# High and low input parts in one product of 512 moving columns, summed when a bank is taken

## The reference

```python
def conv_ffn(h, w_gu, conv_w, conv_b, w_down):
    a, u = jnp.split(h @ w_gu, 2, axis=-1)
    a = causal_depthwise_conv(a, conv_w, conv_b)
    return (jax.nn.silu(a) * u) @ w_down
...
o = from_q_groups(o) @ w_o          # the mixer's output projection
x = x + conv_ffn(h, ...)            # D_MODEL 1024, D_FF 2816
```

## Time and profile before

| | |
|---|---|
| median of 3 runs | 1273.48 us (1270.31 to 1273.67) |
| the profiled execution | 1273.24 us, of which the profiled span is 1271.4 us |
| busy in the span | PE 94%, weight loads 89%, DVE 60%, ACT 44%, POOL 36% |
| up steps of layer 0 | about 236 to 358 us of the span |
| down parts of layer 0 | about 358 to 422 us |
| the same of layer 1 | about 533 to 723 us |
| the same of the third | about 1058 to 1255 us |

### The profile page before, as it was taken

How to read it: one execution, slowest core, us unless ns; L and a number is a source line. 1 busy time by engine, 2 the same in 40 slices (tenths; PEclk the granted TensorE clock), 3 DMA queues, 4 the chain that set the end, 5 groups by cost and what they waited for, 6 DMA issues and landing times.

```text
span 1271.4 us, 23862 instructions
## 1 busy us (share of the span) xinstructions
PE 1195.2 (94%) x9313; PEld 1130.8 (89%) x9313; DVE 765.0 (60%) x1093; ACT 565.6 (44%) x788; POOL 452.6 (36%) x430
## 2 busy tenths in 40 slices
PE   6998999999999888999999999998988898999996
PEld 5987678999999875999999998988978896999996
DVE  5753564767655566676765464436755657777544
ACT  4232344554544444455454336644353444545432
POOL 4522232266630433166651211113431303666401
PEclk9998799999999989999999999998999999999998
DMA  6651001666645540466665453243341453667551
GB/s 200 205 192 41 9 26 34 200 176 188 188 160 183 164 134 2 120 178 187 177 197 182 149 173 127 69 129 104 101 133 34 148 165 87 191 174 196 180 169 50
DMA packets 224581, 175.49 MB, mean 138 GB/s; under 512 B 7796, under 2 KB 205788, under 8 KB 224380
## 3 DMA queue, kind: packets, MB, share of 16 engines
q1 hardware_dynamic: 219052, 168.33, 44.4%
q10 hardware_dynamic: 5424, 6.09, 1.4%
q0 software_dynamic: 32, 0.03, 0.0%
HBM read 173.39 MB, written 1.05 MB: 137 GB/s over the span
## 4 chain that ended last, share of the span: by engine, by line
PE 81%; DVE 8%; ACT 3%; issue 3%; POOL 3%; DMA 1%; SPq 0%; ACTq 0%; DVEq 0%; POOLq 0%
PE bank L574 22%; PE bank L580 22%; PE bank L575 21%; PE bank L840 2%; DVE w_l L1512 2%; ACT w_h L1157 2%; PE bank L608 2%; PE bank L614 1%; PE bank L704 1%; PE bank L1013 1%; PE bank L808 1%; POOL work L2261 1%; DVE work L1627 1%; PE bank L848 1%; PE bank L692 1%
## 5 line engine op out<-in xcount | busy, mean ns | idle before, releaser
L574 PE MATMUL bank<-xh,w_h 128*128 128x256 f32 (+2 forms) x1792 | 451.6, 289 | 5.5 <-DVE xl L1530 4.1
L575 PE MATMUL bank<-xl,w_h 128*128 128x256 f32 (+2 forms) x1792 | 443.0, 284 | 0.0
L574 PEld LDWEIGHTS bank<-xh,w_h 128*128 128x128 f32 x1792 | 339.9, 190 | 8.5 <-issue 5.1
L575 PEld LDWEIGHTS bank<-xl,w_h 128*128 128x128 f32 x1792 | 340.8, 190 | 1.0
L1512 DVE TENSOR_TENSOR w_l<-raw,w_h 128x2048 fp32r<-128x2048 f32 (+3 forms) x95 | 212.2, 2234 | 158.6 <-ACT w_h L1157 158.5
L1157 ACT ACTIVATE w_h<-raw 128x2048 fp32r<-128x2048 f32 (+3 forms) x95 | 173.3, 1825 | 241.7 <-PE bank L580 220.5
L580 PE MATMUL bank<-xh,w_l 128*128 128x256 f32 (+2 forms) x1792 | 251.4, 283 | 2.9 <-DVE w_l L1512 2.9
L580 PEld LDWEIGHTS bank<-xh,w_l 128*128 128x128 f32 x1792 | 230.5, 189 | 3.3 <-DVE w_l L1512 3.1
L2183 POOL TENSOR_TENSOR work<-work 128x256 f32<-128x256 f32 x66 | 162.9, 2469 | 140.4 <-ACT work L1300 140.4
L1795 DVE TENSOR_TENSOR w_l<-raw,w_h 128x2048 fp32r<-128x2048 f32 x66 | 151.4, 2293 | 14.0 <-ACT w_h L1296 13.8
L574 PE MATMUL bank<-hid_h,w_h 128*128 128x256 f32 (+1 forms) x592 | 148.0, 284 | 2.5 <-issue 1.8
(11 more groups left out here) (291 smaller groups left out, 1595.9 us busy)
## 6 DMA issues: line engine op xcount, KB each, us to landing
raw<-in_ffn_w_gu SPq DMA_DIRECT2D x88, 512.0 KB, 5.0
raw<-in_w_in SPq DMA_DIRECT2D x26, 1024.0 KB, 5.2
raw<-in_ffn_w_down SPq DMA_DIRECT2D x40, 512.0 KB, 4.6
raw<-in_w_ffn_up SPq DMA_DIRECT2D x22, 512.0 KB, 4.1
raw<-in_w_ffn_gate SPq DMA_DIRECT2D x22, 512.0 KB, 5.3
raw<-in_nsa_w_in SPq DMA_DIRECT2D x10, 1024.0 KB, 5.4
raw<-in_w_ffn_down SPq DMA_DIRECT2D x20, 512.0 KB, 4.4
raw<-in_swa_w_qkv SPq DMA_DIRECT2D x5, 1024.0 KB, 5.3
```

The costliest lines, as they stand in the source:

```text
L574: mm(dst, parts[0][:, k, cols], high, start=first, stop=False)
L575: mm(dst, parts[0][:, k, cols], low, start=False, stop=False)
```

## The change

Where a stage works on 256 tokens (both output projections of the first block, the up steps of its two layers, and the down parts of all three layers), one product moves 512 columns past each high block: the 256 high parts of x, and beside them the 256 low parts. They go to the two halves of the bank (`side_terms`). The low terms still move 256 columns and add to the left half. The high and low parts of x, of the attention output and of the hidden values are laid out so that one access pattern reaches both; sizes and places stay as they are. The other stages (the input projections, the third layer's up steps, the second block's output projections) keep two products.

Whoever takes a chunk now has to add the two halves, and one instruction of DVE may read only one operand of the accumulator memory here. In the up steps of layers 0 and 1 ACT first copies the right half to a new buffer `f_t` (`side`, two copies a step), DVE adds the left half to it, and a further DVE instruction multiplies the sum by `rstd`, in place. ACT's first tap then waits for that product (`a_scaled`), and the copy of `u`'s right half stands between the first tap and `high`. POOL waits for `u_scaled`. In the output projections and down parts DVE adds the left half to `xT` and then the right half, with a wait for its own first instruction between them (third layer: a copy, then an add).

```diff
@@ -176,7 +176,8 @@
-        xh, xl = sb("xh", [128, KC, T2], F32R), sb("xl", [128, KC, T2], F32R)
+        x_hl = sb("x_hl", [128, 2, KC, T2], F32R)
+        xh, xl = x_hl[:, 0], x_hl[:, 1]
@@ -258,6 +260,7 @@
+        f_t = cv(2, 2, T1)
@@ -569,18 +573,24 @@
+            def high_terms(dst, parts, k, cols, high_low, first):
+
+                mm(dst, parts[0][:, k, cols], high_low[:, 0], start=first, stop=False)
+                mm(dst, parts[0][:, k, cols], high_low[:, 1], start=False, stop=False)
+
+            def side_terms(dst, parts, k, cols, high_low, first):
+
+                mm(dst.rearrange("p (s t) -> p s t", s=2), parts[0][:, k, cols], high_low, start=first, stop=True,
+                   skip_group_check=True)
+
+            def low_terms(dst, parts, ks, cols, high, last, wide=False):
 
                 for k, kx in ks:
-                    ins = mm(dst, parts[1][:, k, cols], high[:, kx, :], start=False, stop=last and (k, kx) == ks[-1])
+                    ins = mm(dst, parts[1][:, k, cols], high[:, kx, :], start=False,
+                             stop=wide or last and (k, kx) == ks[-1], skip_group_check=wide)
                 return ins
 
@@ -589,11 +599,14 @@
-                    high_terms(bank[bank_of(n)][0:M, t0:T], parts, k, slice(128 * c, 128 * c + M), source[0][:, k, t0:T],
-                               source[1][:, k, t0:T], k == 0)
+                    if wide:
+                        side_terms(bank[bank_of(n)], parts, k, slice(128 * c, 128 * c + M), source[:, :, k, 0:T], k == 0)
+                    else:
+                        high_terms(bank[bank_of(n)][0:M, t0:T], parts, k, slice(128 * c, 128 * c + M), source[:, :, k, t0:T],
+                                   k == 0)
@@ -905,12 +918,15 @@
-                            high_terms(bank[q0 + q][:, a:t1], parts, k, slice(128 * q, 128 * q + 128), xh[:, k, a:t1],
-                                       xl[:, k, a:t1], k == 0)
+                            if l < 2:
+                                side_terms(bank[q0 + q], parts, k, slice(128 * q, 128 * q + 128), x_hl[:, :, k, a:t1], k == 0)
+                            else:
+                                high_terms(bank[q0 + q][:, a:t1], parts, k, slice(128 * q, 128 * q + 128), x_hl[:, :, k, a:t1],
+                                           k == 0)
                         if q == 0:
@@ -928,10 +945,10 @@
-                                high_terms(dst, parts, k - k0, cols, hh[:, k, :], hl[:, k, :], k == 0)
+                                side_terms(bank[down_bank(44 + 4 * g + c)], parts, k - k0, cols, both[:, :, k, :], k == 0)
...
-                            last = low_terms(dst, parts, [(k - k0, k) for k in range(k0, k1)], cols, hh, k1 == FC)
+                            last = low_terms(dst, parts, [(k - k0, k) for k in range(k0, k1)], cols, hh, k1 == FC, True)
@@ -1286,11 +1303,25 @@
-                def step(k, n, p, w0, b, slab, target, m, first):
-                    act.wait_ge(proj_taken, n + 1)
+                def step(k, n, p, w0, b, slab, target, m, first, q0):
+
+                    def side(q):
+                        act.wait_ge(proj_done, n + 1 + q)
+                        if not first:
+                            act.wait_ge(proj_taken, n + q - 3)
+                        fn(f_t[:, q, p, :], bank[q0 + q][:, T:2 * T], ACT.Copy).then_inc(side_copied, 1)
+
+                    if l < 2:
+                        side(0)
+                    if l < 2:
+                        act.wait_ge(a_scaled, k + 1)
+                    else:
+                        act.wait_ge(proj_taken, n + 1)
                     if not first:
                         act.wait_ge(conv_mid, k - 1)
                     fn(f_c1[:, p, 0:T], f_a[:, p, 0:T], ACT.Identity, scale=w0, bias=b).then_inc(c1_ready, 1)
+                    if l < 2:
+                        side(1)
                     act.wait_ge(raw_loaded[slab], target)
                     act.wait_ge(proj_done, n + 2)
                     fn(w_h[:, m, :], raw[:, slab, :], ACT.Copy).then_inc(w_hi, 1)
@@ -1740,11 +1771,14 @@
+                b = bank[bank_of(n)]
                 if bias is None:
-                    line.put(V.tensor_tensor(xT[:, c, 0:T1], bank[bank_of(n)][:, 0:T1], xT[:, c, 0:T1], ALU.add), proj_taken)
+                    line.put(V.tensor_tensor(xT[:, c, 0:T1], b[:, 0:T1], xT[:, c, 0:T1], ALU.add))
                 else:
-                    line.put(V.scalar_tensor_tensor(out=xT[:, c, 0:T1], in0=bank[bank_of(n)][:, 0:T1], scalar=vec(bias, c),
-                                                    in1=xT[:, c, 0:T1], op0=ALU.add, op1=ALU.add), proj_taken)
+                    line.put(V.scalar_tensor_tensor(out=xT[:, c, 0:T1], in0=b[:, 0:T1], scalar=vec(bias, c),
+                                                    in1=xT[:, c, 0:T1], op0=ALU.add, op1=ALU.add))
+                line.settle()
+                line.put(V.tensor_tensor(xT[:, c, 0:T1], b[:, T1:2 * T1], xT[:, c, 0:T1], ALU.add), proj_taken)
 
             def add_residual(n0, bias, norm, after):
@@ -1775,13 +1809,26 @@
-                    V.tensor_tensor(f_a[:, p, 2 + T - (t1 - t0):2 + T], bank[b][:, t0:t1], rstd[:, t0:t1], ALU.mult)\
-                        .then_inc(proj_taken, 1)
+                    if l < 2:
+                        dve.wait_ge(side_copied, 2 * k + 1)
+                        V.tensor_tensor(f_a[:, p, 2:2 + T], bank[b][:, 0:T], f_t[:, 0, p, :], ALU.add).then_inc(proj_taken, 1)
+                        dve.wait_ge(proj_taken, n + 1)
+                        V.tensor_tensor(f_a[:, p, 2:2 + T], f_a[:, p, 2:2 + T], rstd[:, t0:t1], ALU.mult).then_inc(a_scaled, 1)
+                    else:
+                        V.tensor_tensor(f_a[:, p, 2 + T - (t1 - t0):2 + T], bank[b][:, t0:t1], rstd[:, t0:t1], ALU.mult)\
+                            .then_inc(proj_taken, 1)
                     dve.wait_ge(proj_done, n + 2)
                     if not first:
                         dve.wait_ge(hid_full, k - 1)
-                    V.tensor_tensor(f_u[:, p, 0:T], bank[b + 1][:, u0:t1], rstd[:, u0:t1], ALU.mult).then_inc(proj_taken, 1)
-                    dve.wait_ge(proj_taken, n + 2)
+                    if l < 2:
+                        dve.wait_ge(side_copied, 2 * k + 2)
+                        V.tensor_tensor(f_u[:, p, 0:T], bank[b + 1][:, 0:T], f_t[:, 1, p, :], ALU.add).then_inc(proj_taken, 1)
+                        dve.wait_ge(proj_taken, n + 2)
+                        V.tensor_tensor(f_u[:, p, 0:T], f_u[:, p, 0:T], rstd[:, u0:t1], ALU.mult).then_inc(u_scaled, 1)
+                        dve.wait_ge(a_scaled, k + 1)
+                    else:
+                        V.tensor_tensor(f_u[:, p, 0:T], bank[b + 1][:, u0:t1], rstd[:, u0:t1], ALU.mult).then_inc(proj_taken, 1)
+                        dve.wait_ge(proj_taken, n + 2)
@@ -2105,7 +2152,15 @@
-            down(2, lambda c: copy_chunk(N_FFN[2] + 44, c, 0, T1))
+            def sum_chunk(c):
+                n = N_FFN[2] + 44 + c
+                dve.wait_ge(proj_done, n + 1)
+                b = bank[bank_of(n)]
+                line.put(V.tensor_copy(xT[:, c, 0:T1], b[:, 0:T1]))
+                line.settle()
+                line.put(V.tensor_tensor(xT[:, c, 0:T1], b[:, T1:2 * T1], xT[:, c, 0:T1], ALU.add), proj_taken)
+
+            down(2, sum_chunk)
```

More of the change, by code:

```diff
@@ L570, in split, with chunk @@
                 return view(w_h, m % 2, k, n), view(w_l, m % 2, k, n), m
-            def high_terms(dst, parts, k, cols, high, low, first):
-                mm(dst, parts[0][:, k, cols], high, start=first, stop=False)
-                mm(dst, parts[0][:, k, cols], low, start=False, stop=False)
-            def low_terms(dst, parts, ks, cols, high, last):
+            def high_terms(dst, parts, k, cols, high_low, first):
[5 more added lines that the diff above has]
+            def low_terms(dst, parts, ks, cols, high, last, wide=False):
                 for k, kx in ks:
-                    ins = mm(dst, parts[1][:, k, cols], high[:, kx, :], start=False, stop=last and (k, kx) == ks[-1])
+                    ins = mm(dst, parts[1][:, k, cols], high[:, kx, :], start=False,
+                             stop=wide or last and (k, kx) == ks[-1], skip_group_check=wide)
                 return ins
-            def chunk(parts, c, K, M, T, ready=None, source=(xh, xl), t0=0):
+            def chunk(parts, c, K, M, T, ready=None, source=x_hl, t0=0, wide=False):
                 n = line["n"]
@@ L652, in opening @@
                                 pe.wait_ge(xl_ready, 8 * stream + k + 1)
-                            high_terms(bank[bank_of(n + c)][:, t0:T], parts, k, slice(128 * c, 128 * c + 128), xh[:, k, t0:T],
-                                       xl[:, k, t0:T], k == 0)
+                            high_terms(bank[bank_of(n + c)][:, t0:T], parts, k, slice(128 * c, 128 * c + 128), x_hl[:, :, k, t0:T],
+                                       k == 0)
                     if half:
@@ L886, in out_proj @@
```

(14 more changed lines are left out.)

31 lines of the change are left out of this document (17 added, 14 removed).

## The result

| | before | changed |
|---|---|---|
| median of 4 runs | 1271.89 us (1267.74 to 1273.67) | 1306.58 us (1303.21 to 1307.19) |
| profiled execution / its span | 1273.24 / 1271.4 us | 1303.21 / 1301.4 us |

The ratio is 1.0272 (1.0239 to 1.0305): slower by 34.7 us in the medians.

The account below looks back on a forecast made before the run. TensorE bounds the kernel (81% of the chain), but a DVE-ACT ring would take over the up steps: +34.8 for these, -5.4 for faster products, +4.5 for last adds, 33.9 on 1273.24 us: 1307 us, range 1282 to 1330.

Parts of the forecast that it names:

- The ring `low`, `a`, first tap, copy, `u`, taps, `low`: Up steps, layers 0 and 1: DVE-ACT order lengthens from 5.35 to 6.49 us and sets the step instead of TensorE.
- The rival by which TensorE stays the late engine: Up steps: ring still fits under TensorE's step, so the change is faster, 1266 us; chance 0.07.
- The up step: 6.49 predicted: Up steps, layers 0 and 1: a step takes 6.49 us in place of 5.68; bounds 5.89 and 7.0.
- ACT's branch: Up steps: ACT's copy, `high`, then `low` take 2.26 us after the copy's start against 2.44 by DVE, so hidden.
- The wide product: 0.225 predicted: TensorE: a 512-column product takes 0.225 us, saving 0.0117 on each pair; bounds 0.216 and the cost of two small ones.
- no cheaper than two: Wide products cost what two small ones do, so the down parts' 5.4 us are gone: 1312 us; chance 0.08.
- the one by which a second half of the columns rides along in the first's time: Wide products take the first half's 0.118 us; down parts give 55 us instead of 5.4: 1257 us; chance 0.02.
- Output projections and first up steps: +3.3 predicted: First block, each layer, end of attention to second `low` of the up steps: +3.3 us; up steps' start slips 2.0.
- The ring of two chunks: First block's output projections: `low`, adds, ACT's squares and `high` close a round of 6.98 us for two chunks and a slab.
- The first four adds of a layer: Down parts, layers 0 and 1: counted as covered ahead of a `low`; uncovered they would cost 1.8 us more.
- TensorE's busy share: Up steps of layers 0 and 1: predicted sign, under 0.9, with TensorE waiting for `w_hi` or `w_lo`.
- that rival: Up steps: waits lower TensorE's clock to 1.2 GHz, a step about 10.6 us, total near 1471 us; chance 0.04.

Follow-up runs that it names:

- copy_first: Changed kernel with only ACT's copy of u's right half moved ahead of the first tap in layers 0 and 1's up steps: 1297.62 us, ratio 1.0159.
- wide_only: Wide products of the change with the elementwise work of the kernel before, right half of each bank never read: 1271.61 us, ratio 0.998.
- down_first4: Kernel with only the down parts changed, but in layers 0 and 1 the right half added only for the first four of eight chunks: 1274.86 us, ratio 1.0017.
- two_small: Changed kernel with each product of 512 columns given as two of 256 into the same bank halves: 1304.37 us, ratio 1.0239.
- down_last4: Kernel with only the down parts changed, but in layers 0 and 1 the right half added only for the last four chunks: 1281.93 us, ratio 1.0048.
- down_only: Only the down parts of all three layers changed, the rest as in the kernel before: 1284.07 us, ratio 1.0079.

## Why the prediction was right, and where it was off

- **Verdict, mechanism, place.** Slower, as forecast; on the size see the bullets below, for its closeness is in part luck. The ring `low`, `a`, first tap, copy, `u`, taps, `low` is what sets the up steps (copy_first moves it by one copy); the third layer's up steps, which the change leaves alone, keep 5.69 us. The rival by which TensorE stays the late engine is out: ahead of the add of `u` DVE waits for ACT's copy, not for TensorE.
- **The up step: 6.49 predicted, 6.14 measured.** This term was mis-sized, by 0.35 us, 14 us over 40 steps. Piece by piece (predicted, measured): `low` to add 2.21, 2.20; add to product 0.65, 0.45; product to first tap 0.68, 0.76; to the copy 0.51, 0.51; to the add of `u` 0.42, 0.39; to its product 0.65, 0.46; to the second tap 0.34, 0.35; third tap 0.63, 0.62; `low` 0.40, 0.40. Two pieces failed, both DVE waiting for itself. I took the 0.23 us that the earlier trace rows show between `u` and the second tap for the price of such a wait. Between add and product it is 0.03 and 0.04 us (0.45 and 0.46 less 0.42), as in the written-out steps, which the prediction had only as a bound. An instruction that follows another on DVE is not at one price. In the kernel before, the last written-out step of the third layer and the first step of its loop run the same three instructions, `u` and the two taps, one after the other:

```profile
1075.59 0.43 DVE L1783 TENSOR_TENSOR work<-bank,rstd 128x256 f32<-128x256 f32 x1 [1.05 <-PE bank L580]
1076.05 0.48 DVE L1786 SCALAR_TENSOR_TENSOR work<-work,vecs 128x256 f32<-128x256 f32 x1
1076.57 0.49 DVE L1791 SCALAR_TENSOR_TENSOR work<-work,vecs 128x256 f32<-128x256 f32 x1
...
1081.28 0.42 DVE L1783 TENSOR_TENSOR work<-bank,rstd 128x256 f32<-128x256 f32 x1 [1.05 <-PE bank L580]
1081.94 0.48 DVE L1786 SCALAR_TENSOR_TENSOR work<-work,vecs 128x256 f32<-128x256 f32 x1 [0.24 <-DVE work L1783]
1082.58 0.48 DVE L1791 SCALAR_TENSOR_TENSOR work<-work,vecs 128x256 f32<-128x256 f32 x1 [0.15 <-DVE work L1786]
```

  Written out they stand 0.03 and 0.04 apart, in the loop 0.24 and 0.15. So for these the price goes with the loop, and yet add and product have the small one in the loop too. What makes that difference no run settles. Against it, the product on two SBUF operands took 0.51 in `a` (0.42 in `u`), 0.09 more than taken, where the upper bound allowed 0.5 more.
- **ACT's branch** was predicted to hide by 0.18. It is level: copy to `high` to `low` 0.26 + 1.96 = 2.22 us, DVE's own way 0.39 + 0.46 + 0.35 + 0.62 + 0.40 = 2.22. By these rows DVE's instructions between the copy and `low` could not have shortened the step by being faster; those ahead of the first tap could.
- **The wide product: 0.225 predicted, 0.2325 and 0.233 (0.93 / 4) measured.** The step "the stream of columns sets the distance and 0.1183 is 0.1067 for 256 columns and 0.0116 besides" failed. The three sizes give 0.462 ns a column at 256, 0.461 at 272, 0.454 to 0.455 at 512: the cost goes all but by the column, and two products of 256 less one of 512 leave 0.004 us to save. The difference between 256 and 272 columns (0.0071) rested on two rounded distances and could not carry that split. So the rival "no cheaper than two", at 0.08, is the truer account of the products, and the one by which a second half of the columns rides along in the first's time, at 0.02, is out. The saving of 5.4 us in the down parts is not there: a slab takes four chunks of 1.41, 5.65 us, as before, and not 5.49. From last `low` to `rstd` the third layer took 65.43 us before, 65.00 in wide_only and 65.68 changed: +0.25 and not the -1.3 predicted, of which the adds are 0.7, predicted 0.8. (From the second slab on a layer has 160 pairs, not 144, and the start of the up steps was carried forward 0.06 us too late; neither matters.) The Trainium skill (TensorE: Matmul & The Clock Gate, section Back-to-back issue gap) has N/2.4 + 2.5 ns, 0.216 us at 512 columns; the bf16 products of the earlier trace rows agree, the float ones here do not, nor with its 131 ns.
- **Output projections and first up steps: +3.3 predicted, +3.2 and +3.5 measured.** The ring of two chunks came out at 6.96 us (`low` at 213.45, 220.41, 227.37), predicted 6.98; in layer 1, whose add has a bias, 7.08.
- **The first four adds of a layer** "lie ahead of a `low` that has a slab's 5.5 us to be there". True in layer 0. In layer 1 the next `low` is in time as well, but the one behind it is not, because DVE has other work in front of it: 1.7 us. The sum named the 1.8 as the price if uncovered, but I looked at one layer's order and used it for both.
- **TensorE's busy share** was to fall under 0.9 in the up steps. It shows 0.975, and the wait stands with the weight loads. The clock did not fall there (1.00 in both layers), so that rival is out.
- **The rest.** 14.0 too much in the steps, 5.4 for products that save nothing and 1.7 for the adds give 33.9 - 14.0 + 5.4 + 1.7 = 27.0 of the measured 30.0. The other 3 us are made of both signs: -2.2 and +3.4 in stretches that the change doesn't touch, 0.9 for the pause ahead of the third layer's up steps, 1.4 with the granted clock of 0.98 in layer 1's down parts, and -0.5 in small differences.

## What to carry to other kernels

Before saving work on the late engine, walk the ring of the others through one step: here 0.33 us of slack a step stood against added instructions that led the ring through a copy, both instructions on `u` and two taps, and no saving on TensorE could reach the end. A product that is wider, with the same columns in all, saves nothing worth having if its cost goes by the column: compare the distances at two widths far apart before counting on a fixed cost. Where adds are put in front of a long queue on DVE, look at each layer's own queue, and if a loop is bound by a ring, try the order of the engine first: moving one copy gave back 0.28 us a step.

## What the runs showed of the hardware

- fp32r products with 128x128 weights come 0.118 us apart at 256 columns, 0.125 at 272 and 0.2325 at 512, all in stretches with a granted clock of 1.00 (the 2.4 GHz level); bf16 ones 0.216 at 512.
- The same instructions take a different time from one execution to the next, by the granted clock. The stretch from layer 1's `rstd` to the end of the second block's mixers is the same code in every kernel here. It took 312.5 us at a granted clock of 0.99 (wide_only), 315.0 at 0.98 (down_first4), 316.7 at 0.97 (before), 320.1 at 0.96 (changed, two_small, down_last4) and 324.0 at 0.95 (down_only). Two windows of the kernel before inside it:

```profile
933.10:953.10 20.00, 16.14 (x110) 13.63 (x108) 10.24 (x14) 12.95 (x13) 3.73 (x2) 1.00 0.32 106
953.10:973.10 20.00, 17.84 (x125) 16.16 (x124) 6.80 (x10) 7.42 (x16) 0.00 (x0) 1.00 0.03 7
```

and the same place in the changed kernel:

```profile
958.40:978.40 20.00, 16.14 (x85) 13.25 (x84) 7.20 (x13) 13.52 (x14) 3.72 (x2) 0.85 0.31 104
978.40:998.40 20.00, 20.00 (x101) 18.52 (x101) 3.06 (x7) 1.49 (x2) 0.00 (x0) 0.64 0.00 1
```

TensorE was busy for 19.89 of 20 us before them and for 16.14 in the first in both, with the same waits (the longest 2.4 us), and yet in one execution the clock stayed at 1.00 and in the other it fell, to 0.85 and then 0.64 in the mean. What decides it no run here shows. It is worth up to 11 us in this stretch alone, more than every effect here but the up steps, so a part of the change that is worth 2 us is read from its own stretch, at the same clock, and not from the total.
